# A hybrid decoder trunk: the scan inputs' SiLU as one ScalarE activation instead of tanh and a VectorE pass

## The reference, cut to what matters

```python
def hybrid_layer(x, ...):
    h = rms_norm(x, norm_g)
    u = h @ w_in
    c_q, c_kv, k_pe, g_mla, u_conv, g_conv, z, xbc, dt_raw = jnp.split(u, offs, axis=-1)
    o_mla = mla_mixer(...) * jax.nn.silu(g_mla)
    o_conv = conformer_conv_mixer(...) * jax.nn.silu(g_conv)
    o_ssd = ssd_mixer(z, xbc, dt_raw, ...)
    return x + jnp.concatenate([o_mla, o_conv, o_ssd], axis=-1) @ w_out

def ssd_mixer(z, xbc, dt_raw, conv_w, conv_b, ...):
    xbc = jax.nn.silu(causal_depthwise_conv(xbc, conv_w, conv_b))   # 4 taps, 1280 channels
    ...
    decay = jnp.exp(jnp.where(causal, seg, -jnp.inf))               # the scan uses exp
    ...
```

## Time and profile before

| What | Value |
|---|---|
| Time, median of 3 runs | 1581.65 us (1581.61 to 1582.94) |
| The profiled execution, own time | 1583.54 us |
| Its span, first to last instruction | 1581.7 us |
| TensorE busy | 1543.9 us (98%) |
| VectorE busy | 1009.4 us (64%) |
| ScalarE busy | 690.7 us (44%) |
| Table loads on ScalarE | 67, 86.0 us |
| Granted TensorE clock, mean | 0.995 |

### The profile page before, as it was taken

The page is one execution under the profiler, slowest core; times in us unless marked ns, Lnnn a source line. Parts: engine busy times, 40 slices in busy tenths (PEclk is TensorE's granted clock), DMA queues, the critical chain, the costliest instruction groups (busy, mean ns, idle before and its releaser), DMA issues.

```text
span 1581.7 us, 18434 instructions
## 1 busy us (share of the span) xinstructions
PE 1543.9 (98%) x7062; PEld 1229.3 (78%) x7062; DVE 1009.4 (64%) x1496; ACT 690.7 (44%) x1014; POOL 44.6 (3%) x86
## 2 busy tenths in 40 slices
PE   7999999999999999999999999999999999999997
PEld 6777777777788887788887877777777887878885
DVE  7544674889988877443454456658898978762321
ACT  7455543334356645222254455433444565452110
POOL 0000000000000000110000000000000000001100
PEclk9999999999999999999999999999999999999999
DMA  5322232122233233544432222222212232235441
GB/s 221 93 90 81 94 91 70 67 67 67 72 111 108 85 93 96 166 143 145 140 100 83 86 81 97 76 67 74 73 67 87 93 121 101 78 107 162 147 136 64
DMA packets 44423, 158.13 MB, mean 100 GB/s; under 512 B 5520, under 2 KB 5808, under 8 KB 44336
## 3 DMA queue, kind: packets, MB, share of 16 engines
q1 hardware_dynamic: 36720, 129.64, 25.3%
q0 software_dynamic: 6464, 23.12, 5.1%
q10 hardware_dynamic: 1152, 4.19, 0.7%
HBM read 148.50 MB, written 8.44 MB: 99 GB/s over the span
## 4 chain that ended last, share of the span: by engine, by line
PE 83%; DVE 9%; ACT 5%; issue 1%; DMA 1%; ACTq 0%; DVEq 0%; POOL 0%; POOLq 0%
PE acc L493 18%; PE acc L495 18%; PE acc L494 18%; PE S L498 6%; PE S L493 3%; PE S L495 3%; PE S L494 3%; PE T L495 3%; PE T L493 3%; PE T L494 3%; DVE wlo L1010 2%; PE O L498 2%; ACT L733 1%; PE T L632 1%; DVE hlo L1093 1%
## 5 line engine op out<-in xcount | busy, mean ns | idle before, releaser
L493 PE MATMUL acc<-hhi,whi 128*128 128x512 f32 (+1 forms) x1504 | 601.8, 400 | 14.1 <-DVE wlo L1010 13.5
L1010 DVE TENSOR_TENSOR wlo<-stage,whi 128x1024 fp32r<-128x1024 f32 (+2 forms) x252 | 300.8, 1197 | 453.9 <-ACT whi L745 451.6
L495 PE MATMUL acc<-hhi,wlo 128*128 128x512 f32 (+1 forms) x1504 | 588.8, 392 | 0.0
L494 PE MATMUL acc<-hlo,whi 128*128 128x512 f32 (+1 forms) x1504 | 588.5, 391 | 0.0
L745 ACT ACTIVATE whi<-stage 128x1024 fp32r<-128x1024 f32 (+2 forms) x252 | 260.1, 1036 | 446.3 <-PE acc L495 227.8
L493 PEld LDWEIGHTS acc<-hhi,whi 128*128 128x128 f32 (+1 forms) x1504 | 282.7, 188 | 78.8 <-DVE wlo L1010 15.1
L495 PEld LDWEIGHTS acc<-hhi,wlo 128*128 128x128 f32 (+1 forms) x1504 | 282.4, 188 | 62.1
L494 PEld LDWEIGHTS acc<-hlo,whi 128*128 128x128 f32 (+1 forms) x1504 | 282.9, 188 | 60.2 <-issue 2.9
L1065 DVE SCALAR_TENSOR_TENSOR cacc<-glu,pv,cacc 128x512 f32<-128x512 f32 x240 | 171.7, 749 | 4.7
L733 ACT ACT_TABLE_LOAD x67 | 86.0, 1283 | 7.4 <-issue 5.1
L733 ACT ACTIVATE prob<-S,cols 128x128 f32<-128x128 f32 (+3 forms) x48 | 25.3, 528 | 117.7 <-DVE cols L1269 117.7
(11 more groups left out here) (229 smaller groups left out, 1557.7 us busy)
## 6 DMA issues: line engine op xcount, KB each, us to landing
stage<-weights SPq DMA_DIRECT2D x236, 512.0 KB, 3.4
y_features<-xg POOLq DMA_DIRECT2D x32, 256.0 KB, 4.1
acsb<-acs_rows POOLq DMA_DIRECT2D x16, 384.0 KB, 4.1
xg<-x_features ACTq DMA_DIRECT2D x8, 512.0 KB, 9.5
xr<-x_features POOLq DMA_DIRECT2D x16, 256.0 KB, 4.2
xr<-y_features POOLq DMA_DIRECT2D x16, 256.0 KB, 4.1
stage<-weights SPq DMA_DIRECT2D x8, 256.0 KB, 2.6
stage<-weights SPq DMA_DIRECT2D x4, 384.0 KB, 3.0
```

The lines of the kernel that those rows point to most:

```text
L493: nc.tensor.matmul(out, a, c, start=start, stop=False)
L494: nc.tensor.matmul(out, a, d, start=False, stop=False)
L495: return nc.tensor.matmul(out, b, c, start=False, stop=stop)
L1010: nc.vector.tensor_tensor(wlo[u % RING][:, 0:w], stage[u % STAGE][:, 0:w], whi[u % RING][:, 0:w].bitcast(F32), ALU.subtract).then_inc(lo_d ...
```

## The change

The SiLU of the ten `xbc` tiles of each layer becomes one ScalarE activation, in place in `xb`; the product on VectorE and the halving of taps and biases are gone. A new signal `xb_in` takes the place of `tanh_in` there, and ScalarE itself signals `xb_ready`. Behind the Silu of n = 15, 17, 19 and 21 in attention, ScalarE takes the exponential of one column of ones into an unused column (`exp_table`).

```diff
-        cols = sb("cols", [P, 32])
+        cols = sb("cols", [P, 36])
...
+                def xb_silu(i):
+
+                    act.wait_ge(xb_in.sem, xb_in.at(layer, i + 1))
+                    a(xb_ready, xb[i // 5][:, i % 5, :], xb[i // 5][:, i % 5, :], ACT.Silu)
+
+                def exp_table():
+
+                    nc.scalar.activation(cols[:, 35:36], ones[:, 0:1], ACT.Exp)
...
                             if not finished_in_attention(args[0]):
-                                tanh(1.0, xb[i // 5][:, i % 5, :])
+                                xb_silu(i)
...
                         if n % 2 == 1 and finished_in_attention((n + 27) // 2):
                             i = TILES[(n + 27) // 2][1]
-                            tanh(1.0, xb[i // 5][:, i % 5, :])
+                            xb_silu(i)
+                            if n + 1 < 24:
+                                exp_table()
...
-                    ts(None, par("scw", 0, 10 * SSD_K + 10), par("scw", 0, 10 * SSD_K + 10), 0.5, ALU.mult)
...
                     for k in range(3):
-                        stt(tanh_in if k == 2 else None, o, raw[:, k:k + SEQ], par("scw", SSD_K * ch + k), o,
+                        stt(xb_in if k == 2 else None, o, raw[:, k:k + SEQ], par("scw", SSD_K * ch + k), o,
                             ALU.mult, ALU.add)
-                    silu(xb_ready, o, o)
+                    if taps_open[0]:
+                        convolve(1)
```

More of the change, by code:

```diff
@@ L350, in hybrid_kernel @@
         lat_r = sig("lat_r", 2)
-        tanh_done = sig("tanh_done", 6 + 4 + 10 + 4 + 6)
-        tanh_in = sig("tanh_in", 6 + 4 + 10 + 4 + 6)
+        tanh_done = sig("tanh_done", 6 + 4 + 4 + 6)
+        tanh_in = sig("tanh_in", 6 + 4 + 4 + 6)
+        xb_in = sig("xb_in", 10)
         kd_ready = sig("kd_ready", 1)
@@ L408, in hybrid_kernel @@
         tap_done = sig("tap_done", 4 * CONV_K)
-        counted = (rx_ready, lat_sq, lat_r, tanh_done, tanh_in, kd_ready, kr_half, kr_both, dt_asked, dt_exp, da_ready,
+        counted = (rx_ready, lat_sq, lat_r, tanh_done, tanh_in, xb_in, kd_ready, kr_half, kr_both, dt_asked, dt_exp, da_ready,
                    acs_ready, acs48_ready, proj_taken, sq_part, sq_ready, head_r, qk_ready, max_ready, exp_done,
@@ L787, in latent_hi, with tanh @@
                     nc.scalar.activation(hi[:, i, :], temp[:, :], ACT.Identity, scale=par(g, i)).then_inc(cq_hi.sem, 1)
-                def tanh(scale=1.0, src=None):
+                def tanh():
                     tanhs[0] += 1
                     act.wait_ge(tanh_in.sem, tanh_in.at(layer, tanhs[0]))
-                    a(tanh_done, temp2[:, :], temp[:, :] if src is None else src, ACT.Tanh, scale=scale)
+                    a(tanh_done, temp2[:, :], temp[:, :], ACT.Tanh)
+                def xb_silu(i):
[3 more added lines that the diff above has]
+                    nc.scalar.activation(cols[:, 35:36], ones[:, 0:1], ACT.Exp)
                 for name, args, own in STEPS:
```

## The result

The changed kernel takes 1603.46 us (median of 4 runs, 1602.3 to 1605.22) against 1582.3 us of the kernel before measured beside it: a ratio of 1.0135, 95% interval 1.0119 to 1.0151. It is slower, as forecast (1598.4 us), and 0.46 us beyond the upper end of the range. The profiled execution of it took 1602.62 us, with a span of 1600.8 us, 19.1 us more than before. The medians lie 21.2 us apart, so the two profiled executions show 2.1 us less than they do.

What follows compares the result with a forecast made beforehand. TensorE, 98% busy, bounds the kernel, fed by a ScalarE and VectorE relay without rest. A layer loses 9.01 - 0.72 + 0.10 = 8.39 us, both 16.8 us: 1598.4 us against the 1581.65 us median; range 1588 to 1603 us.

Steps and rivals of the forecast that it cites:

- What bounds the kernel: Whole kernel: TensorE is 98% busy; the ScalarE and VectorE relay runs at nearly its pace, with 0.91 us room at n = 23.
- The block of two loads: Attention, n = 15, 17, 19, 21: two table loads, one-column exponential and gaps make whi 2.75 us later each time.
- 9.01 us: Attention, by n = 23: TensorE's lateness in each layer, from a relay 9.87 us late, plus 0.05, less 0.91 us room.
- its own sign: Profile after: TensorE waits for prob at n = 16, 18, 20, 22, some 18 us beside the old 3.5; otherwise prediction wrong.
- VectorE's product: Ten products of 0.69 us a layer go; only the one before the last attention output gains, 0.72 us a layer.
- The load behind n = 23: End of attention, fifth tile: Silu's one load falls where ScalarE waits for TensorE, so it costs nothing.
- Loads in the SSD part: SSD part: Silu's loads hidden, exponentials' loads make the relay 1.44 us late; TensorE waits 0.10 us in chunk 3.
- The clock: Behind new TensorE stalls: slow clock may cost up to 1.7 us a layer; nothing in the sum, 3.4 us in the range.
- rival D: Last stall of each layer: slow clock behind it adds 1.7 or 3.4 us, giving 1600.1 or 1601.8 us; chance 0.22.
- A: Attention: first load hidden in ScalarE's wait for the taps, block 1.45 us, 3.19 us a layer, 1588.0 us; chance 0.10.
- B: Attention: ScalarE's idle time takes both loads, only the gain at its end is left, 1580.2 us; chance 0.05.
- C: Attention: a drain makes each table switch 2.66 us, block 5.51 us, about 20.8 us a layer, 1623 us; chance 0.03.

Runs made afterwards that it cites:

- the copies in the kernel before: Kernel before with eleven one-column ScalarE copies behind its tanh of n = 15, 17, 19, 21: 1603.1 us, ratio 1.0130; with six copies 1591.44 us.

## Why the prediction was right or wrong, point by point

*What bounds the kernel.* Right. The relay of ScalarE and VectorE has no rest, and its lateness reaches TensorE less the room: the copies in the kernel before show it without the change.

*The block of two loads.* Right: 2.66 us measured for 2.75, first load behind the taps, no drain. The stalls stand at the four places forecast. The stall itself, "9.01 us" a layer, measured 8.4 and 8.3; a block of 2.66 us instead of 2.75 makes 8.65 of it by the same steps, and the last 0.3 us stay open. By its own sign, that TensorE's new waits for `prob` add up to some 18 us, the prediction was wrong: they are 12.8 us. What it left out of that sign is its own remark that slow clock behind a stall shortens the next wait, 1.7 us in each layer.

*VectorE's product.* The gain of 0.72 us a layer was there in layer 1 (the wait went from 2.29 to 1.56 us) and mostly lost in layer 0 (2.29 to 2.04 us). The step that failed is "The load behind n = 23 ... Nothing": it looked at ScalarE, which does wait for TensorE there, and not at VectorE. VectorE at this place in the kernel before, and in the changed one, up to the output that the earlier trace rows has for the kernel before:

```profile
425.18 1.22 DVE L1010 TENSOR_TENSOR wlo<-stage,whi 128x1024 fp32r<-128x1024 f32 x1 [1.43 <-ACT whi L745]
```

```profile
429.00 1.23 DVE L1022 TENSOR_TENSOR wlo<-stage,whi 128x1024 fp32r<-128x1024 f32 x1 [2.34 <-ACT whi L746]
430.14 2.73 DVE L1077 SCALAR_TENSOR_TENSOR cacc<-glu,pv,cacc 128x512 f32<-128x512 f32 x4
432.80 1.22 DVE L1022 TENSOR_TENSOR wlo<-stage,whi 128x1024 fp32r<-128x1024 f32 x1
...
438.68 0.68 DVE L1004 TENSOR_TENSOR xg<-O,xg 128x512 f32<-128x512 f32 x1
```

Before, VectorE waited 1.43 us at the second of these `wlo`; now it comes to it late, with no idle time, and the output starts some 0.5 us later against TensorE than forecast. In layer 1 TensorE was itself held up by slow clock behind n = 22, which gives VectorE that time back. The other runs bear it out: where Silu's load at n = 23 is on ScalarE's path and no slow clock stands ahead of the output (the exponential's column left out), TensorE waits 2.0 us in both layers; where that load is covered or isn't there (Silu's load early, both covered, Silu in the SSD part alone), it waits 1.57 us in both.

*Loads in the SSD part.* Right that next to nothing is lost: 0.10 us a layer was forecast, and in layer 1, where no slow clock disturbs it, TensorE needs 52.83 us from the attention output to the fourth chunk in both kernels. And with Silu only there the kernel is no slower.

*The clock.* The mechanism was right, but its size was "nothing" in the sum and came out as 1.7 us net in the profiled execution. The rival D, slow clock behind the last stall of each layer (1600.1 or 1601.8 us), is nearer to what happened than the forecast, but is still below the 1603.46 us; one of its two stretches came behind the wait for the attention output.

*What was missing.* No step of the prediction speaks of `cols` growing from 32 to 36 columns. It was in the diff, I took it for room and no more, and it moved every operand behind it: about 2.5 us, measured as 2.9 us by the medians (2.0 us by the profiled spans) by putting it back. The step that failed is the sum, "16.8 us", from which this term is absent; in it the clock, too, stands at nothing. In the terms of the profile: 16.7 us of relay (18.0 forecast), 1.0 us gained (1.4 forecast), 2.5 us of addresses (0), 1.7 us of clock (0), 0.7 us less at the start, which differs from run to run (the wait at 95 us lies between 94.77 and 95.93 us in the traces): 19.2 us, against 19.1 of the spans. The relay came out 1.3 us cheaper than forecast, which hid a part of what was left out; addresses and clock together add 4.2 us, and that is why the time came out above 1603. That the addresses alone are enough to leave the range is shown by the changed kernel with nothing moved: 1600.6 us, all its four runs (1599.04 to 1601.25 us) inside the range. With 2.5 us more in the sum the forecast would have been 1600.9 us. The other 2.5 us to the median aren't laid out by a trace: the kernel before itself measured 0.65 us more beside the changed one than the 1581.65 us on which the forecast stood, and the rest is most likely clock.

*The rivals.* A (1588 us) is not what the change does. It is what comes out once Silu's load is put where ScalarE waits (1587.6 us); with the other load off the relay it is 1589.7 us. B is what happens once both loads are covered. C, the drain of the Trainium skill (ScalarE: Activation LUTs, What ACT_TABLE_LOAD costs), is ruled out for these loads: 0.01 to 0.02 us stand between load and next activation in each of the rows above, and 2.66 us is the price of both loads and the column together, not that of one switch.

## What to carry to other kernels

Read the room of a relay at the point of use (end of the producer against start of the consumer, step by step), and the waits in which it can catch up; busy shares hide both. A table load costs by what is queued behind it (with every address kept, 32 more of them gave a ratio of 1.0113 in one place and 0.9985 in another): put it where the engine waits anyway, and look in the order which wait the compiler has put on the load itself. When a diff widens a buffer, ask what it moves.

## What the runs showed of the hardware that was not expected

A matmul of float32r with 512 columns takes 389 or 392 to 396 ns by the address of the operand it streams, with moves of 32, 64 and 128 bytes; 32 bytes put in between `cqhi` and `ckvhi` raised the matmuls of `ckvhi` to 395 to 398 ns and left those of `cqhi` at 389 to 390. Which addresses are good is open. Waits of TensorE of 1.7 to 2.35 us are sometimes followed by a stretch at the lower clock of 1.2 GHz, which costs 1.7 us by the windows above, and sometimes not: the wait of 1.72 us at n = 0 is followed by a clock of 0.72 in the kernel before and of 1.00 in the changed one.
